# Three PSUM copies moved ahead of a square root, and a table load and stores moved at the end of a two-block kernel

## The reference

```python
# block 1
h = rmsnorm(x, pre_norm_g)
q, k, v, g_attn, x_lru, g_lru = split(h @ w_in)
y_attn = rmsnorm(diff_attention(q, k, v, lam), subln_g) * (1 - lam_init) * silu(g_attn)
r, gi = sigmoid(xc @ w_r + b_r), sigmoid(xc @ w_i + b_i)       # xc: causal convolution of x_lru
log_a = -8 * r * softplus(-lam_param); a = exp(log_a)
h_lru = scan(a, sqrt(max(-expm1(2 * log_a), 0)) * gi * xc)      # the square root
x = x + rmsnorm(concat(y_attn, h_lru * silu(g_lru)) @ w_out, post_norm_g)
# block 2
h = x + mixed(x)                              # a recurrence and sparse attention
h = h + peer_ffn(rmsnorm(h))                  # 8 heads x 16 experts per token, rows gathered
gate = sigmoid(rmsnorm(h, ple_gate_norm) @ ple_gate_w)
out = h + (p @ ple_proj) * gate               # the last gate
```

## Time and profile before

| | |
|---|---|
| time, median of 3 runs | 1081.5 us (1080.64 to 1082.86) |
| the profiled execution | 1080.88 us, its span 1079.0 us |
| PE busy | 985.2 us, 91% |
| PE weight loads | 555.3 us, 51% |
| DVE busy | 694.7 us, 64% |
| ACT busy | 467.7 us, 43% |
| POOL busy | 309.3 us, 29% |
| moved by DMA | 347.31 MB, mean 322 GB/s |
| mean granted PE clock | 0.986 |

### The profile page before, as it was taken

One profiled execution on the slowest core, in us unless ns is written; L12 is line 12 of the kernel. 1 busy time (PEld: TensorE's weight loads), 2 busy tenths in 40 slices (PEclk: granted clock), 3 DMA queues, 4 the chain that ended last, 5 costly groups with the idle time before them and its releaser, 6 DMA issues.

```text
span 1079.0 us, 11375 instructions
## 1 busy us (share of the span) xinstructions
PE 985.2 (91%) x3829; PEld 555.3 (51%) x3829; DVE 694.7 (64%) x1576; ACT 467.7 (43%) x1211; POOL 309.3 (29%) x307
## 2 busy tenths in 40 slices
PE   8998999999999998999999799998798997877787
PEld 7998658544785475644454353555333432321122
DVE  5879656214453489787676676767667778755555
ACT  1253356111353247554644444355434455633344
POOL 4000000000000033545544434454324345433340
PEclk9999999999999999999999899999989999999999
DMA  8435442334627279999999999999999999999993
GB/s 329 167 134 220 156 156 78 104 131 176 242 80 296 113 279 422 421 414 421 422 421 421 421 422 422 420 421 421 421 421 422 422 421 412 421 422 422 421 421 121
DMA packets 46650, 347.31 MB, mean 322 GB/s; under 512 B 5088, under 2 KB 6496, under 8 KB 9088
## 3 DMA queue, kind: packets, MB, share of 16 engines
q0 software_dynamic: 37584, 269.89, 60.4%
q1 hardware_dynamic: 8928, 76.66, 18.9%
q10 hardware_dynamic: 80, 0.03, 0.0%
HBM read 345.25 MB, written 1.05 MB: 321 GB/s over the span
## 4 chain that ended last, share of the span: by engine, by line
PE 53%; DMA 28%; DVE 10%; ACT 7%; issue 2%; POOL 0%; SPq 0%; DVEq 0%; ACTq 0%; POOLq 0%
PE pp L1240 14%; DMA xc_rg<-in_peer_uv,small 11%; DMA kT<-in_peer_uv,lamt 6%; PE pp L782 5%; DMA ig<-in_peer_uv,small 4%; PE pp L778 4%; DMA spare<-in_peer_uv,small 4%; PE pp L740 3%; PE pp L699 3%; PE pp L909 3%; PE pp L929 3%; PE pp L887 3%; PE pp L1126 2%; PE pp L1237 2%; PE pp L736 2%
## 5 line engine op out<-in xcount | busy, mean ns | idle before, releaser
L1745 ACT ACTIVATE small<-small 128x1 f32<-128x1 f32 x256 | 51.6, 201 | 309.8 <-DVE small L2557 308.8
L1763 ACT ACTIVATE diag<-ident,small 128x128 f32<-128x128 f32 x216 | 86.7, 402 | 7.1
L1753 ACT ACTIVATE small<-small 128x1 f32<-128x1 f32 x216 | 63.6, 294 | 7.8
L1240 PE MATMUL pp<-sm,diag 128*128 128x512 f32 x108 | 54.8, 632 | 12.8 <-ACT diag L1763 12.8
L1240 PE MATMUL pp<-gl,diag 128*128 128x512 f32 x108 | 53.3, 617 | 11.1 <-ACT diag L1763 11.1
L593 POOL IOTA tail<- 128x256 int32 x1 | 0.3, 342 | 214.9 <-DVE xs L2160 214.9
L1240 PE MATMUL pp<-kT,diag 128*128 128x512 f32 x108 | 53.7, 620 | 8.6 <-ACT diag L1763 8.6
L1240 PE MATMUL pp<-ig,diag 128*128 128x512 f32 x108 | 54.1, 625 | 7.5 <-ACT diag L1763 7.5
L651 POOL DMA_INDIRECT ig<-in_peer_uv,small x27 | 32.9, 1217 | 98.0 <-PE pa L1191 53.6
L1240 PE MATMUL pp<-xc_rg,diag 128*128 128x512 f32 x108 | 53.3, 617 | 8.1 <-ACT diag L1763 8.1
L782 PE MATMUL pp<-hT,ring 128*128 128x256 f32 x256 | 58.1, 381 | 0.0
(11 more groups left out here) (607 smaller groups left out, 2163.0 us busy)
## 6 DMA issues: line engine op xcount, KB each, us to landing
ring<-in_wall SPq DMA_DIRECT2D x31, 2048.0 KB, 7.7
ring<-in_wall SPq DMA_DIRECT2D x3, 512.0 KB, 8.5
ring<-in_wall SPq DMA_DIRECT2D x1, 1280.0 KB, 9.8
xs<-in_x SPq DMA_DIRECT2D x2, 512.0 KB, 3.7
post_g<-in_rows POOLq DMA_DIRECT2D x2, 512.0 KB, 7.6
tail<-in_wall SPq DMA_DIRECT2D x1, 1024.0 KB, 10.9
kT<-in_wall SPq DMA_DIRECT2D x1, 1024.0 KB, 12.9
lt<-in_sub_keys SPq DMA_DIRECT2D x1, 1024.0 KB, 8.1
```

What stands on the lines that cost most here:

```text
L1240: return nc.tensor.matmul(acc[t][:, c, :], diag[:, n * P:(n + 1) * P], rows_uv[page_of(g)][:, D + c * HALF:D + (c + 1) * HALF], start=Fals ...
L1745: nc.scalar.activation(acts[:, at:at + BATCH], dots[:, at:at + BATCH], ACT.Gelu_apprx_tanh)\
L1753: ins = nc.scalar.activation(wk[:, g % LAG:g % LAG + 1], acts[:, g % LAG:g % LAG + 1], ACT.Copy, scale=probs[:, g:g + 1] if g < PAIR_FROM else
L1763: nc.scalar.activation(diag[:, n * P:n * P + words], ident[:, :] if g < PAIR_FROM else two_idents, ACT.Copy, scale=wk[:, g % LAG:g % LAG + ...
```

## The change

Three edits. Of v0's seven copies on ACT the first three now stand ahead of the square root, the other four behind it. After `side_std(1)` ACT has one more activation, a sigmoid of one column (128x1) into a column of `stat` that nothing reads later, ahead of the wait for `scaled`. Of the four last stores SP issues the two of the lower partitions, ACT the two of the upper ones, each after the wait for its part.

```diff
             for n, (a, b) in enumerate(LAST_PARTS):
                 sp.wait_ge(s["y_made"], 4 + n)
-                for c in range(2 if n == 0 else 1):
-                    sp.dma_start(out[P + SIDE:2 * P, c * HALF + a:c * HALF + b], last_y[SIDES[c], a:b])\
-                        .then_inc(s["stored"], 16)
+                sp.dma_start(out[P + SIDE:2 * P, a:b], last_y[LOW, a:b]).then_inc(s["stored"], 16)
             sp.wait_ge(s["stored"], 16 * (2 + 2 * len(LAST_PARTS)))
...
             for i in range(7):
                 part("k1", i)
+            for i in range(3):
+                part("v0", i)
             act.wait_ge(s["mult_sq"], 1)
             nc.scalar.activation(lt[:, :], lt[:, :], ACT.Sqrt, scale=2.0).then_inc(s["mult_made"], 1)
-            for name in ("v0", "v1"):
-                for i in range(7):
-                    part(name, i)
+            for i in range(3, 7):
+                part("v0", i)
+            for i in range(7):
+                part("v1", i)
...
             side_std(1)
+
+            nc.scalar.activation(stat[:, 61:62], eps_col, ACT.Sigmoid)
             act.wait_ge(s["scaled"], 2 * NT + 3)
...
-            act.wait_ge(s["y_made"], 3 + len(LAST_PARTS))
-            a, b = LAST_PARTS[-1]
-            act.dma_start(out[P + SIDE:2 * P, HALF + a:HALF + b], last_y[HIGH, a:b]).then_inc(s["stored"], 16)
+            for n, (a, b) in enumerate(LAST_PARTS):
+                act.wait_ge(s["y_made"], 4 + n)
+                act.dma_start(out[P + SIDE:2 * P, HALF + a:HALF + b], last_y[HIGH, a:b]).then_inc(s["stored"], 16)
```

## The result

| | before | after |
|---|---|---|
| median | 1081.24 us (1079.46 to 1082.95, 6 runs) | 1075.05 us (1074.53 to 1076.01, 6 runs) |
| profiled execution | 1080.88, span 1079.0 | 1076.01, span 1074.1 |

The ratio is 0.9942, 95% interval 0.9929 to 0.9955: 6.2 us less, between 4.9 and 7.7. The two profiled executions differ by 4.87, so the median gained some 1.3 us more than this pair of profiles shows.

A forecast was written before the change was run, and what follows sets the result against it. PE was taken to bound 122 to 330 us, DMA 390 to 1056 us. Gains of 3.15 (copies) and 1.2 (end) sum to 4.35, taking 1080.88 to 1076.5 profiled; forecast 1077.1 us, range 1075.3 to 1079.6.

The forecast's parts named there:

- PE's pause: Ahead of v0's fifth product PE waited for ACT's copies; moving three ahead of the root was to gain 3.15 us.
- second step: Whole kernel: before's median lay 0.6 above its profiled execution; carrying that over turned 1076.5 into about 1077.1 us.
- D: Experiments' theory, not the prediction's: in many executions the pause lowers PE's clock, costing 1.7 us that the copies also save.
- rival (c): At 118 to 330 us, unbroken PE work lowers the clock and the kernel gets slower, one spell giving 1087; chance 0.04.
- The third copy and the table load ahead of the root: On ACT: copy done about 99.86, load at 101.15, 0.6 us before the root's input; root stays at 101.75.
- The seventh product: Of v0 on PE: its bank's copy, behind the root, frees it at 104.09, its turn is 104.46; not late by 0.4.
- rival (a): The front gain is lost in the DMA-bound gathers, 420 becoming 418 GB/s: 1080.3 us, no measurable difference; chance 0.11.
- rival (b): At the end the sigmoid's load isn't moved ahead of the wait, or a second is made: 1078.0 us; chance 0.05.
- The end: Added sigmoid and split last stores together: 1.2 us less, bounds 0.97 to 1.5; the last sum 0.97 earlier.
- The term behind it: From last sum to end: the last stores land 2.0 us (SP) and 2.3 us (ACT) after their start, the end at 1077.8.
- The prediction's other estimate: Last stores: by the skill, fixed cost about 2.0 us plus 0.08 for 32 KB on either engine; end gain 1.4.
- The drain behind a table load: At the end's sigmoid: the skill adds about 1.38 us to the load's 1.28; prediction said the trace shows none.

The follow-up runs named there:

- e1: Kernel before with only the three copies of v0 moved ahead of the root: 1076.72 against 1081.25 us, ratio 0.9964.
- e2: Kernel before with only the added sigmoid and the last stores split over two queues: 1080.06 against 1081.25 us, ratio 0.9985.
- e6: Kernel before with an unused ACT copy after the root, making PE's pause about 1 us longer: 1083.5 against 1081.9 us, ratio 1.0015.
- e7: Kernel before with e6's unused copy and 28 unused PE transposes in the pause: 1081.06 against 1081.9 us, ratio 0.9991.
- e8: Kernel before, unchanged, run again as a kernel of its own: 1081.01 against 1081.9 us, ratio 0.9995.
- e10: Changed kernel with the last stores as before, three on SP and one on ACT: 1075.52 against 1075.25 us for the changed kernel beside it.
- e9: Changed kernel without the added sigmoid: 1076.69 against 1075.25 us for the changed kernel beside it.
- e5: Kernel before with 18 unused PE transposes in the pause ahead of v0's fifth product: 1080.12 against 1081.9 us, ratio 0.9982.

## Why the prediction was right in its direction and short by two microseconds

**The term that was mis-sized: PE's pause.** The prediction booked 3.15 us, what the pause's own length moves the sixth product by. That number held to 0.02: the first gather came 3.17 earlier relative to the root's input in after and 3.13 in e1. What it left out is what the pause does behind itself. In an execution in which the clock falls, the matmuls after it lose 1.7 us (e2's rows; 1.74 by the first gathers of e6 and e7), and removing the pause removes that too. 3.15 + 1.7 + 1.4 = 6.25 where the clock falls and 4.55 where it doesn't; the medians of 6.2, 5.7 and 6.4 between changed kernel and before on three sets of runs lie nearer to the first, the pair of profiles (4.87, with 0.15 of it from an earlier start) near the second. The profile of before happened to be an execution without the fall. How often the clock falls in before is inferred from the medians, not seen.

The forecast took a second step that failed with it: it set before's median 0.6 above its profiled execution and carried that over to after, where the median lies 0.96 below (1075.05 against 1076.01). Of the 2.05 us between forecast and median 1.5 lie in that step and 0.5 in the profiled execution itself (1076.5 was forecast for it). Both profiled executions were late at the root's input (99.43 and 99.28), nine of the other eleven were there by 98.36. Taken to about 98.2, the profiled execution of after would have been near 1074.9, its median; that of before near 1079.6, 1.6 us below its median of 1081.24 (e8's profile, early and without the fall, has 1079.22). This is an estimate from the table's column "root input". It agrees with D, by which most executions of before hold 1.7 us for the clock and those of after none.

The step that failed is rival (c), "the pause isn't what keeps it up", with the clock of 1.00 in the pause as its evidence. The question was put the wrong way round. I asked if work without the pause could bring the clock down, and not if the pause does, so the term for it stood at nothing. The Trainium skill, TensorE: Matmul & The Clock Gate, Part 1, says that idle time between bursts of matmuls can put the clock back from 2.4 to 1.2 GHz. e2 and e6 agree, with the clock at 0.67 and 0.57 behind the pause, and so does e7, with 1.00; the two profiled executions of before did not show it. It should have been a rival on the faster side: the pause costs more than its length in executions that this profile isn't one of. With the 1.7 us that e2 measured later, that rival gives 1075.4.

**Confirmed.** The third copy and the table load ahead of the root: load over at 101.00, 0.60 before the root, which kept its place. The seventh product was not late, v1's copies waited for k1's join until 110.64 at no cost, and the first scores moved by all of it. The gather stretch handed the shift on undiminished (664.78 in after, 664.97 in before), so rival (a) fell; the sigmoid's load came ahead of the waits, so rival (b) fell.

**The end**: 1.2 was booked, 1.41 came (1.00 up to the last sum, 0.41 behind it). The last sum is 1.0 earlier as worked out (0.97), with PE the new bound: the second sigmoid waits 1.10 us for it. The term behind it was 0.2 low because ACT's 32 KB store landed in 2.1 us, not 2.3; the same store took 2.0 in e10 and 2.2 in e9, so before's 2.3 was not a fixed price of ACT's queue. The prediction's other estimate, 1.4 with one price of about 2.1 us for either queue, is nearer in the sum, though the two queues did not land alike (1.8 on SP, 2.1 on ACT). The share of the split stores in it is small next to the sigmoid's (e10). The drain behind a table load, which the Trainium skill (ScalarE: Activation LUTs, What ACT_TABLE_LOAD costs) adds, is not on the path in after (0.01 us from load to activation) or in e9 (0.02 us).

No kernel here beats the changed one beyond what the timing can tell.

## What to carry to other kernels

A pause of PE in a stretch where PE sets the time costs its length and sometimes the slow matmuls behind it (1.7 us behind the 2.92 us here); so price it with both, and look at the clock behind it in more than one execution. When a kernel's times spread more than a variant's over as many executions (3.4 us against 1.9 in e5), look for something that happens in some executions only. Copies that free another engine's buffers belong ahead of an instruction that still waits for its input, and a table load belongs into idle time ahead of a wait; each is worth what the engine behind it then can't hide, as PE hid 0.3 us of the load.

## What the runs showed of the hardware

The same pause of 2.92 us ended with the clock at 1.00 twice and at 0.67 (104 to 108 us) once; with 3.87 us of idling it was 0.57, the fifth product taking 3.64 us; with 1.47 us, or with matmuls in the pause and 0.73 to 0.86 us of idling left, it was 1.00. Transposes whose output nothing reads, put into the pause, were worth 2.4 us with the longer pause (e7 against e6) and 1.4 us with the pause as it was (e5 against 44 executions of before, 0.7 to 2.1). What decides between the two ends of the same pause stays open. The first 98 us differ by up to 1.9 us between executions of the same work, with the clock at 1.00 up to 90 us in all 13 profiles; most of it is there when PE's first matmuls with weights begin (7.50 to 9.29 us). A table load took 1.28 us, and the activation behind it began 0.01 to 0.02 us after its end.
